# Routing of the tokens by pairs of token tiles, with the row stores on ScalarE's queue, in a hybrid block with a mixture of 32 experts

## The reference, cut to what matters

```python
h = h + (g_a * y_a + g_b * y_b) @ w_out[l]
hn = rmsnorm(h, norm_ffn_g[l])
# hierarchical_moe(hn, ...):
glog = xf @ w_rg + b_rg                      # 4 groups, the best one is taken
elog = (xf @ w_re + b_re)[chosen group]      # 8 experts in it, the best two
combine = one_hot(eid) * softmax(topv) * pg
for e in range(32):
    h = silu(xf @ w_gate[e]) * (xf @ w_up[e])
    y = y + combine[:, e:e + 1] * (h @ w_down[e])
```

## Time and profile before

| what | value |
|---|---|
| median of 3 runs | 897.65 us (897.07 to 899.61) |
| profiled execution | 897.03 us |
| span in the profile | 895.3 us |
| PE busy | 848.3 us, 95% |
| DVE, ACT busy | 428.0 us, 231.9 us |
| DMA | 250.03 MB, mean 279 GB/s |
| chain that ended last | PE 84%, DMA 10%, DVE 3% |

### The profile page before, as it was taken

The page is one execution under the profiler, slowest core; times in us unless marked ns, Lnnn a source line. Parts: engine busy times, 40 slices in busy tenths (PEclk is TensorE's granted clock), DMA queues, the critical chain, the costliest instruction groups (busy, mean ns, idle before and its releaser), DMA issues.

```text
span 895.3 us, 11458 instructions
## 1 busy us (share of the span) xinstructions
PE 848.3 (95%) x4635; PEld 550.1 (61%) x4635; DVE 428.0 (48%) x824; ACT 231.9 (26%) x423; POOL 7.6 (1%) x24
## 2 busy tenths in 40 slices
PE   8999999999999999999999969999995799999885
PEld 7888888877777888888844334544531443644532
DVE  5538325677675344436769144135133334335133
ACT  6322222464444222213304121100110100110124
POOL 0000000000000100000000000000000000000000
PEclk9999999999999999999999979999996999999998
DMA  8544312212222743696999999999999999999994
GB/s 292 153 94 112 102 48 94 94 48 76 67 94 57 216 136 94 236 388 245 367 383 346 415 429 428 425 427 428 427 429 428 426 428 428 427 426 428 428 410 191
DMA packets 72408, 250.03 MB, mean 279 GB/s; under 512 B 23032, under 2 KB 46624, under 8 KB 59168
## 3 DMA queue, kind: packets, MB, share of 16 engines
q1 hardware_dynamic: 71984, 248.18, 71.3%
q0 software_dynamic: 288, 1.05, 0.3%
q10 hardware_dynamic: 80, 0.02, 0.0%
HBM read 245.04 MB, written 4.20 MB: 278 GB/s over the span
## 4 chain that ended last, share of the span: by engine, by line
PE 84%; DMA 10%; DVE 3%; ACT 1%; issue 1%; SPq 0%; DVEq 0%; ACTq 0%
PE bank L1024 18%; PE bank L708 9%; PE bank L710 9%; PE bank L709 9%; PE bank L1083 8%; DMA R<-w_down 5%; DMA R<-w_gate 3%; PE bank L735 2%; PE bank L737 2%; PE bank L736 2%; PE bank L988 2%; PE by_side L988 2%; PE bank L1111 2%; PE bank L1070 2%; PE bank L1112 1%; DMA gate_fifth<-w_gate 1%
## 5 line engine op out<-in xcount | busy, mean ns | idle before, releaser
L1024 PE MATMUL bank<-R,packT 128*64 128x512 f32 (+1 forms) x972 | 187.0, 615 | 14.3 <-DMA R<-w_up 11.4
L1024 PEld LDWEIGHTS bank<-R,packT 128*64 128x64 f32 (+1 forms) x972 | 58.6, 130 | 124.5 <-issue 124.0
L1646 DVE TENSOR_TENSOR wlo<-raw,whi 128x2048 fp32r<-128x2048 f32 x33 | 75.5, 2288 | 84.8 <-ACT whi L1304 84.7
L708 PE MATMUL bank<-xnT_hi,whi 128*128 128x512 f32 x288 | 113.8, 395 | 0.0
L710 PE MATMUL bank<-xnT_hi,wlo 128*128 128x512 f32 x288 | 112.3, 390 | 0.0
L709 PE MATMUL bank<-xnT_lo,whi 128*128 128x512 f32 x288 | 112.2, 390 | 0.0
L1083 PE MATMUL bank<-R,actT 128*64 128x512 f32 (+1 forms) x384 | 75.2, 645 | 13.1 <-DMA R<-w_down 12.8
L1304 ACT ACTIVATE whi<-raw 128x2048 fp32r<-128x2048 f32 x33 | 63.0, 1910 | 66.9 <-PE by_side L710 33.8
L710 PEld LDWEIGHTS bank<-xnT_hi,wlo 128*128 128x128 f32 x288 | 54.1, 188 | 11.4
L708 PEld LDWEIGHTS bank<-xnT_hi,whi 128*128 128x128 f32 x288 | 54.1, 188 | 11.2 <-issue 0.6
L709 PEld LDWEIGHTS bank<-xnT_lo,whi 128*128 128x128 f32 x288 | 54.2, 188 | 10.7
(11 more groups left out here) (416 smaller groups left out, 1329.5 us busy)
## 6 DMA issues: line engine op xcount, KB each, us to landing
R<-w_up SPq DMA_DIRECT2D x27, 2048.0 KB, 21.3
R<-w_gate SPq DMA_DIRECT2D x25, 2048.0 KB, 21.2
R<-w_down SPq DMA_DIRECT2D x21, 2048.0 KB, 22.6
raw<-w_in SPq DMA_DIRECT2D x17, 1024.0 KB, 5.1
R<-w_down SPq DMA_DIRECT2D x12, 1024.0 KB, 13.8
R<-w_gate SPq DMA_DIRECT2D x14, 512.0 KB, 6.6
raw<-w_in SPq DMA_DIRECT2D x20, 256.0 KB, 4.6
R<-w_up SPq DMA_DIRECT2D x5, 1024.0 KB, 9.8
```

Of the source, the lines that this page charges most:

```text
L708: pe.matmul(dst, hi_w, hi_x, start=start, stop=False)
L1024: mm = pe.matmul(dst[s * w:(s + 1) * w, :], packT[:, side, c, s * w:(s + 1) * w], part_of(s, c) if part_of else slots[s // 2].tiles[s % 2] ...
L1646: dve.tensor_tensor(wlo[c % 2][:, :], raw[c % 2][:, :], whi[c % 2][:, :].bitcast(F32), ALU.subtract).then_inc(lo_split, 1)
```

## The change

The routing goes by pairs of tiles. `wide_unit` takes work ahead of any tile: in the last unit `turn_h(0)` stands ahead of tile 2, and `turn_h(1)`, `route(0)` and `route(1)` ahead of tile 3. VectorE reads, chooses and spreads for tiles 0 and 1, and then for 2 and 3; TensorE ranks and gathers a pair at a time. The second pair's inverse root (`norm_h(1)`) stands ahead of the first pair's masks. All copies to `hgT` are ScalarE's. The product with the gain on VectorE and the load of `ffn_g` go: `hn_first` is h times `rstd`, read by ScalarE from `h_tok` through a strided view, and the gain comes in when rows are copied to `packT`. The stores of rows are issued by ScalarE behind its scalings and not by SyncE. SyncE's load of `gate_fifth` waits for the third mask and not for the first. The banks change to suit. The core of the diff:

```diff
-                    for dst, src in ((ffn_g[:, :], norm_ffn_g[0].partition_broadcast(P)),
-                                     (w_router[:, :, 0:NG], w_router_group[0].rearrange("(c p) n -> p c n", p=P)),
+                    for dst, src in ((w_router[:, :, 0:NG], w_router_group[0].rearrange("(c p) n -> p c n", p=P)),
...
-            for t in range(TT):
-                sp.wait_ge(hn_ready, t + 1)
-                sp.dma_start(hn_rows[1 + t * P:1 + (t + 1) * P, :].rearrange("q (a n) -> q a n", a=2),
-                             hn_first[:, :, t, :, :].rearrange("q a c p -> q a (c p)")).then_inc(hn_stored, 16)
...
-            sp.wait_ge(masks_ready, 1)
+            sp.wait_ge(masks_ready, 3)
...
-                    if before_last and t == TT - 1:
-                        before_last()
+                    if t in ahead:
+                        ahead[t]()
...
-                    pe.wait_ge(hgT_a, t - 1)
-                    pe.wait_ge(hgT_b, t - 1)
+                    pe.wait_ge(hgT_copied, 2 * t - 2)
...
+            def rank_tiles(pair):
+
+                pe.wait_ge(hgT_copied, 4)
+                pe.wait_ge(picked_ready, pair + 1)
+                for t in range(2 * pair, 2 * pair + 2):
+                    dst = ranks_psum[:, t * NE:(t + 1) * NE]
+                    pe.matmul(dst, all_ones[:, :], spaced_row[:, :], start=True, stop=False)
+                    for tp in range(t + 1):
+                        mm = pe.matmul(dst, earlier[:, :] if tp == t else all_ones[:, :],
+                                       picked[:, tp, :], start=False, stop=(tp == t))
+                mm.then_inc(ranks_done, 1)
...
+            def route_first_tiles():
+                turn_h(1)
+                pe.wait_ge(router_scaled, 1)
+                route(0)
+                route(1)
...
-            pe.wait_ge(router_scaled, 1)
-            route(0)
+                wide_unit(c, c % 2, mgT_hi, mgT_lo, dve_tile_done,
+                          {2: lambda: turn_h(0), 3: route_first_tiles} if c == UNITS - 1 else ())
+
             turn_h(2)
-            route(1)
+            pe.wait_ge(route_iotas_made, 13)
+            rank_tiles(0)
             turn_h(3)
             route(2)
             route(3)
...
-            keep_warm(3)
-            pe.wait_ge(route_iotas_made, 13)
-            pe.wait_ge(picked_ready, 1)
...
-            def gather_first(n):
-
-                for t in range(TT):
+            def gather_first(pair, n):
+
+                for t in range(2 * pair, 2 * pair + 2):
                     pe.wait_ge(masks_ready, t + 1)
                     for c in range(4):
                         mm = pe.matmul(bank[2 + n][:, c * P:(c + 1) * P], hn_first[:, n, t, c, :], onehot_first[:, t, :],
                                        start=(t == c == 0), stop=(t == TT - 1), skip_group_check=True)
-                mm.then_inc((left_turned, right_turned)[n], 1)
+                if pair:
+                    mm.then_inc((left_turned, right_turned)[n], 1)
...
-            for _ in range(3):
+            pe.wait_ge(h_ready, 2 * TT)
+            pe.wait_ge(hn_ready, 2)
+            for n in range(2):
+                gather_first(0, n)
+            fill(256, 4)
+            rank_tiles(1)
+            for t in range(TT):
+                mm = pe.matmul(bank[6][:, 0:NE], all_ones[:, :], picked[:, t, :], start=(t == 0), stop=(t == TT - 1))
+            mm.then_inc(ranks_done, 1)
+            for _ in range(2):
                 fill(256, 4)
             pe.wait_ge(hn_ready, TT)
-            gather_first(0)
+            gather_first(1, 0)
             number_rows(1, 1)
-            gather_first(1)
+            gather_first(1, 1)
...
+            def copy_hgT(t):
                 act.wait_ge(hgT_psum, t + 1)
-                act.activation(hgT[t // 2][:, 4 * half:4 * half + 4, (t % 2) * P:(t % 2 + 1) * P],
-                               bank[4 + 2 * (t % 2) + half][:, :].rearrange("p (c q) -> p c q", c=4),
-                               ACT.Copy).then_inc(hgT_c if half else hgT_a, 1)
+                for half in range(2):
+                    act.activation(hgT[t // 2][:, 4 * half:4 * half + 4, (t % 2) * P:(t % 2 + 1) * P],
+                                   bank[HGT_BANKS[t][half]][:, :].rearrange("p (c q) -> p c q", c=4),
+                                   ACT.Copy).then_inc(hgT_copied, 1)
+
+            def scale_h(t):
+                act.wait_ge(rstd_ready, t // 2 + 1)
+                act.activation(hn_first[:, :, t, :, :], h_tok[:, t, :].rearrange("q (p a c) -> q a c p", a=2, c=KT // 2),
+                               ACT.Copy, scale=rstd[:, t:t + 1]).then_inc(hn_ready, 1)
+
+            def store_rows(t):
+                act.wait_ge(hn_ready, t + 1)
+                act.dma_start(hn_rows[1 + t * P:1 + (t + 1) * P, :].rearrange("q (a n) -> q a n", a=2),
+                              hn_first[:, :, t, :, :].rearrange("q a c p -> q a (c p)")).then_inc(hn_stored, 16)
...
+            copy_hgT(0)
+            copy_hgT(1)
             square_h(1, 2)
             scale_h(0)
             scale_h(1)
+            store_rows(0)
+            store_rows(1)
+            copy_hgT(2)
             square_h(1, 3)
-            copy_hgT(2, 0)
-            copy_hgT(3, 0)
-            copy_hgT(3, 1)
+            copy_hgT(3)
             scale_h(2)
             scale_h(3)
+            store_rows(2)
+            store_rows(3)
...
+                    act.wait_ge(late_loaded, 16 * 5)
                     act.wait_ge(hn_stored, 16 * (TT + 1))
-                if r < 3:
-                    act.activation(packT[:, 0, 4 * n:4 * n + 4, :], bank[b][:, :].rearrange("p (c q) -> p c q", c=4),
-                                   ACT.Copy).then_inc((main.pack_a, main.pack_b)[n], 1)
-                    return
                 for c in range(4):
-                    last = act.activation(packT[:, 1, 4 * n + c, :], bank[b][:, c * P:(c + 1) * P], ACT.Copy,
+                    last = act.activation(packT[:, r // 3, 4 * n + c, :], bank[b][:, c * P:(c + 1) * P], ACT.Copy,
                                           scale=gain_pc[:, 4 * n + c:4 * n + c + 1])
...
-            for t in range(TT):
-                gain_h(0, t)
...
-            add_h(1, 0)
-            gain_h(1, 0)
-            add_h(1, 1)
-            gain_h(1, 1)
-            norm_h(0)
-            add_h(1, 2)
-            copy_hgT(0)
-            copy_hgT(1)
-            gain_h(1, 2)
-            add_h(1, 3)
-            gain_h(1, 3)
-            copy_hgT(2)
-            norm_h(1)
...
+            def read_logits(t):
+                dve.wait_ge(logits_done, t + 1)
+                dve.scalar_tensor_tensor(out=logits[:, t, :], in0=logits_psum(t), scalar=rstd[:, t:t + 1], in1=b_router[:, :],
+                                         op0=ALU.mult, op1=ALU.add).then_inc(logits_ready, 1)
+
+            def choose(pair):
+
+                ts = slice(2 * pair, 2 * pair + 2)
+                dve.wait_ge(logits_ready, 2 * pair + 2)
+                places(place_g[:, ts, :], glog[:, ts, :], NG)
+                then(dve.scalar_tensor_tensor(out=em[:, ts, :].rearrange("p t (g e) -> p t g e", g=NG),
+                                              in0=place_g[:, ts, :].unsqueeze(3).to_broadcast([P, 2, NG, EPG]), scalar=MASKED,
+                                              in1=elog[:, ts, :].rearrange("p t (g e) -> p t g e", g=NG), op0=ALU.mult, op1=ALU.add))
+                then(dve.tensor_reduce(in_group[:, ts, :], em[:, ts, :].rearrange("p t (g e) -> p t e g", g=NG), AX.X, ALU.max))
+                places(place_8[:, ts, :], in_group[:, ts, :], EPG)
+                then(dve.tensor_scalar(chosen_8[:, ts, :], place_8[:, ts, :], 2.0, None, ALU.is_lt))
+                in_chosen_group(picked[:, ts, :], chosen_8, ts).then_inc(picked_ready, 1)
+
+            def spread_choices(pair):
+
+                ts = slice(2 * pair, 2 * pair + 2)
+                then(dve.tensor_scalar(first_8[:, ts, :], place_8[:, ts, :], 1.0, None, ALU.is_lt))
+                in_chosen_group(sel[:, 0, ts, :], first_8, ts).then_inc(choices_spread, 1)
+                then(dve.tensor_scalar(second_8[:, ts, :], place_8[:, ts, :], 1.0, None, ALU.is_equal))
+                in_chosen_group(sel[:, 1, ts, :], second_8, ts).then_inc(choices_spread, 1)
+
+            def first_masks(pair):
+
+                dve.wait_ge(choices_spread, 4 * pair + 2)
+                dve.wait_ge(ranks_done, pair + 1)
+                pick_rows(ranks, slice(2 * pair, 2 * pair + 2))
+                for t in range(2 * pair, 2 * pair + 2):
+                    dve.tensor_scalar(onehot_first[:, t, :], spaced_iota[:, 0:P], row_first[:, t:t + 1], None,
+                                      ALU.is_equal).then_inc(choices_spread, 1)
+                for t in range(2 * pair, 2 * pair + 2):
+                    dve.wait_ge(choices_spread, 4 * pair + 3 + t % 2)
```

(32 more changed lines are left out.)

132 lines of the change are left out of this document (32 added, 100 removed).

## The result

The changed kernel takes 905.50 us (median of 4 runs, 904.99 to 906.69) where the kernel before takes 898.11 on the same chip (897.07 to 899.61): a ratio of 1.0083 with a 95% interval of 1.0064 to 1.0102, or 7.4 us more. Forecast were 906.0 and slower. Its profiled execution took 905.87 us, 904.0 of them span, 8.7 more than in before (8.84 in device time); the two traces are 0.58 us apart already at 412 us, where SyncE issues the first halves, ahead of the routing.

The account below looks back on a forecast made before the run. Behind the routing the kernel was taken to end when the weights have come in by DMA. Start +6.4, wait -0.4 and clock +2.5 gave +8.5 us on 897.65: 906.1, said as 906, range 899.5 to 909.5.

Parts of the forecast that it names:

- The late halves: SyncE's second halves of three 1 MB loads move from 424.95 to about 428.3; DMA engines stay empty 3.3 us longer.
- The scaling: ScalarE's `scale_h`, reading `h_tok` through the strided view, takes 2.15 us in place of 1.15.
- The stores as a second queue: On ScalarE's queue, stores alternate single packets with the weights and land last, at 452.8 us, holding up `packT`.
- The first rival: Stores get past the weights in longer turns, landing at 446.8; +1.4 us, 899.1 us in all; chance 0.12.
- The start, and the wait that goes: First gate projection starts at about 454.1 against 447.63, +6.4 us; TensorE's wait for `gate_fifth` goes, -0.4.
- The clock at the projection: TensorE, idle from 444.6 to 454.1, starts the first gate projection at half clock: +2.5 us, bounds 0 and 2.9.
- The sum: +6.4 - 0.4 + 2.5 = +8.5 us on TensorE's chain, from the first projection to the DMA hole at 472 us.
- The middle of the routing: Pair gathers take 1.9 us per half; first gather 435.4 to 439.0, last mask 441.0, gather done 444.6.
- the 2.9 us that the change could bring: TensorE's gather by pairs is done at 444.6 and not at 447.5.
- The later rounds: Four copies to `packT` cost 0.5 us more each round, but TensorE waits for weights at 507 us anyway: 0.

Follow-up runs that it names:

- e1: The changed kernel with the four row stores issued by SyncE again, between the second halves and `gate_tail`; 905.11 us, ratio 1.0080.
- e2: The kernel before with only the row stores moved from SyncE's queue to ScalarE's, behind each pair's scalings; 899.08 us, ratio 1.0013.
- e4: The changed kernel with eleven products of 256 columns, no part of the result, behind the last gather; 903.51 us, ratio 1.0059.
- e3: The changed kernel with `route(0)` and `route(1)` behind the last unit's tile 3 and not ahead of it; 903.06 us, ratio 1.0061.
- e8: e6 with first-pair routes behind tile 3, inverse root and last tile's sum before reading first logits, `packT` copy mid-sorting, further reordering; 899.27 us, ratio 1.0014.
- e6: e1 with SyncE issuing `gate_fifth` ahead of R[6] (2 MB); 900.14 us, ratio 1.0019.
- e7: The kernel before with SyncE issuing `gate_fifth` ahead of R[6] (2 MB); 897.95 us, ratio 0.9997.
- e5: The changed kernel with the first pair's masks ahead of the second pair's inverse root; 906.20 us, ratio 1.0089.
- e9: e8 with four products of 256 columns, no part of the result, where TensorE waited for the first masks; 899.95 us, ratio 1.0010.
- e10: e9 with R[6] issued ahead of the wait for the masks and `gate_fifth` again; 898.69 us, ratio 1.0011.

## Why the prediction was right

- **The late halves: right in place, too dear in the reasoning.** They were issued at 429.16 where 428.3 was forecast (0.6 of it is the distance at 412 us). The forecast had nothing to cover them "unless the first stores are early", and the first stores were early. The first went out at 426.59, as soon as the first scaling had ended, while the second scaling ran; the forecast had put both behind both scalings. So the DMA engines were at 389 GB/s from 428 to 429, and `gate_fifth` landed only 0.6 us later than before. e1, without this cover, shows what it hid: `gate_fifth` at 457.4.
- **The scaling: right.** 2.2 us each against 2.15, from the one row of the same view in a later round.
- **The stores as a second queue: right.** Forecast were turns of one packet each and a last landing at 452.8; it was 452.12, early by 0.7, or by 1.3 without the distance at 412 us, as the first stores were moving by 428 and not by 430. The queues of after from 431 to 432 us and from 448 to 449 us (packets, MB, share):

```profile
q1 hardware_dynamic: 29, 0.24, 71.5%
q10 hardware_dynamic: 34, 0.07, 25.8%
```

```profile
q1 hardware_dynamic: 50, 0.13, 35.1%
q10 hardware_dynamic: 57, 0.12, 29.9%
```

29 packets of weights (q1) beside 34 of stores (q10), and 50 beside 57, about as at 486 us in the earlier trace rows, and the same near-even mix in e2 (37 beside 33, from 436 to 437). The counts are near even whatever the sizes. From 431 to 432 us 2 KB packets run against 8 KB ones and get about a quarter of the bytes; from 448 to 449 both are near 2 KB and share evenly; from 444.5 to 445, where R[6] moves in packets of some 16 KB, it is 16 packets beside 14, but 0.25 MB beside 0.02. Even counts over 1 us would also come from longer turns of equal length. Against these stands the start: in e2 the two queues meet at about 427 us, and the three half microseconds from 427.5 on have 16, 19 and 13 packets of the stores beside 16, 12 and 19 of the weights. Nine packets of 8 KB in a row would take an engine 2.8 us by the prediction's 0.31 us each, and such windows would hold nearly one queue alone. The Trainium skill (DMA: Bandwidth & Descriptors, Queues, rings and completion order) has an engine drain a whole packet of some 9 to 17 descriptors of one ring before it switches. The trace doesn't agree if its rows are such descriptors. The first rival, 899.1 us with the last store landed at 446.8, did not come.
- **The start, and the wait that goes: right.** The start moved by 5.9 (forecast 6.4), filling `packT` took 1.14 (1.15), and TensorE no longer waits for `gate_fifth` (-0.44, forecast -0.4).
- **The clock at the projection: right in kind, a little large.** 2.2 us against 2.5; e4 shows it. TensorE stopped at 448.4 and not at 444.6, and the clock fell some 2.8 us behind that, near the 2.9 of the earlier trace rows.
- **The sum.** 5.88 - 0.44 + 2.23 = 7.67 us in the trace against 8.5, and 7.4 in the medians. The forecast of 906.0 was 0.5 us above the result, but that closeness is in part luck: it was built on 897.65, and the kernel before had 898.11 in the comparison. In the change itself the forecast was 1.1 us too large, from the start (0.5), the clock (0.3) and what the medians have less than the traces.
- **The middle of the routing: wrong from 436 us on, and hidden.** The first masks (the gather begins at 435.74, forecast 435.4) and `picked` of the second pair (438.85, forecast 438.6) came as forecast, to 0.4 us. But the first pair's gather took 6.3 us, 435.74 to 442.0, and not 3.6, because the clock was at 0.50 from 434.1 to 440.9 us. The step that failed took the row of four tiles at full clock and halved it. The last masks came at 444.4 and not at 441.0, the gather was done at 448.4 and not at 444.6: later than before (447.7), so the 2.9 us that the change could bring were not there at all. The sorting, behind the masks, ended at 452.60, where the forecast had it some 3.4 us earlier. This cost nothing in after, where the stores landed at 452.1; in e3 VectorE's half was the last condition, and in e8 the slow gather costs 2.4 us of the path.
- **The later rounds: put at 0, not quite.** The four copies to `packT` were to cost nothing there. In the traces the projection at 507 us starts 8.33 us later than in before, where the products ahead of it started 7.78 later (498.53 against 490.75), so 0.5 us was added. The `w_down` load behind it lands 8.0 later.
- **Two readings of the earlier trace rows.** The prediction has TensorE wait 11.47 us for `gate_fifth` and 17.86 us for `w_down`. These are times from issue to landing; TensorE waited 0.44 us for the one and 7.2 us for the other (518.1 to 525.27). The sum used the 0.4, so nothing hangs on it.
- **The weight of one cause: wrong in the experiments' expectations.** e1's expectation had the stores' queue carry about 4.5 of the 7.4 us. In before it is worth 1.0 (e2), undone in after nothing (e1), and 5.6 with one more exchange (e6). The projection starts when the gather is done and ScalarE's half of `packT` is filled, which waits for the stores; its fifth eighth waits for `gate_fifth` and for VectorE's half. The late halves, the stores' queue, R[6] and the clock each push a different one of these, and the prices don't add.

## What to carry to other kernels

Where several loads, stores and results must be there before the next product, write down when each lands and undo them together. An experiment that undoes one only shows the next in line. A small-packet store on a queue of its own takes turns with the weights and lands when they do. That is free if nobody waits for it; here its buffer was the next one to be filled. Of two loads in one queue, the one that is waited for goes first; that was worth 5 us without a byte less in e6 against e1, and nothing in e7, where the load was not late.

## What the runs showed of the hardware that was not expected

**The clock can fall while TensorE is at work.** In after, the two windows around the fall are these:

```profile
434.00:435.00 1.00, 1.00 (x8) 1.00 (x7) 0.86 (x5) 0.74 (x1) 0.00 (x0) 0.55 1.01 418
435.00:440.00 5.00, 4.83 (x23) 4.72 (x24) 4.13 (x20) 3.53 (x2) 0.00 (x0) 0.50 1.01 401
```

TensorE was busy for all of 433 to 435 us and had been for 0.86 of 431 to 432, with turns of 128 columns and routes of 36, and was granted 0.50. Read in windows of half a microsecond from 424 to 445 us, every kernel with pair routing shows such a stretch: 434.1 to 440.9 in after, 433.4 to 443.6 in e3, 434.6 to 441.4 in e8, and a second one in the last token tile or its routes in e1 (425.8 to 429.2), e5, e6, e9 and e10. The kernel before had none in its profiled execution, but e2 and e7, whose TensorE programs are that of before, had one of 3.4 us from 433.4 and 433.7 on, and e9 and e10 with one program for both had 6.9 and 3.4 us of it behind 434 us. So the same products, in the same order, do not always get the same clock. In one profile for each kernel it can't be told how much of this is the kernel and how much the execution, and what decides it stays open; fills ahead of the first gather did not settle it. Its price in e8 is 2.4 us of the routing's path (6.2 against 3.8), nearly the 2.9 that the change could have won.

**A DMA issue on ScalarE held up nothing here.** The first store's issue (521 ns) ran beside the second scaling, and two scalings with a store's issue between them took 4.38 us, and 4.27 in the second pair. In e1, which has no store on ScalarE, they took 4.21 and 4.26, so the issue cost 0.2 us at most.
